# Opening a two-layer transformer kernel in four quarters of 256 features instead of two halves of 512

## The reference, cut to what matters

```
mod = silu(c) @ w_ada[0] + b_ada[0]     # 6 parts of 1024: shift, scale, gate, shift2, scale2, gate2
h   = rmsnorm(x, norm_g[0, 0]) * (1 + scale) + shift
# hgrn2_mixer(h, w_in, ...): 8 heads; w_in has 5 fields of 8 x 128 columns
q, v, zf, zb = (h @ w_in[:, f, head, :] for f in (0, 1, 2, 3))
ff, fb = sigmoid(zf), sigmoid(zb); kf, kb = 1 - ff, 1 - fb
# then a scan over the tokens in both directions, with q, k, v and the forget gates
```

## Time and profile before

| what | value |
|---|---|
| median of 3 runs | 1183.71 us (1177.64 to 1186.02) |
| span of the profiled execution | 1179.7 us |
| the median above that span | 4.0 us |
| TensorE busy in the span | 1110.8 us, 94% |
| VectorE, ScalarE, GpSimd busy | 414.1, 229.0 and 128.1 us |
| moved by DMA | 321.26 MB, 272 GB/s on average |

### The profile page before, as it was taken

One profiled execution on the slowest core, in us unless ns is written; L12 is line 12 of the kernel. 1 busy time (PEld: TensorE's weight loads), 2 busy tenths in 40 slices (PEclk: granted clock), 3 DMA queues, 4 the chain that ended last, 5 costly groups with the idle time before them and its releaser, 6 DMA issues.

```text
span 1179.7 us, 19786 instructions
## 1 busy us (share of the span) xinstructions
PE 1110.8 (94%) x8488; PEld 659.2 (56%) x8488; DVE 414.1 (35%) x1058; ACT 229.0 (19%) x530; POOL 128.1 (11%) x226
## 2 busy tenths in 40 slices
PE   4999999998999999999998899989989899999996
PEld 2666666665444666666563444434545756666552
DVE  2155555655712340000113654307843320000104
ACT  3111101101211411111111311126632311111110
POOL 0343433433100000000002000000000000000003
PEclk9999999999999999999999999999999899999999
DMA  9985444446941579999999942246751499999996
GB/s 345 307 277 157 115 144 144 144 144 216 379 160 67 179 277 422 426 426 426 427 424 339 389 167 76 89 161 215 282 218 44 155 378 429 426 425 424 426 418 228
DMA packets 101888, 321.26 MB, mean 272 GB/s; under 512 B 3985, under 2 KB 39105, under 8 KB 86433
## 3 DMA queue, kind: packets, MB, share of 16 engines
q1 hardware_dynamic: 93296, 298.05, 66.0%
q0 software_dynamic: 3248, 10.87, 2.7%
q10 hardware_dynamic: 5248, 10.98, 2.4%
HBM read 305.73 MB, written 14.16 MB: 271 GB/s over the span
## 4 chain that ended last, share of the span: by engine, by line
PE 74%; DMA 15%; DVE 4%; issue 2%; ACT 2%; SPq 2%; POOL 1%; POOLq 0%; ACTq 0%; DVEq 0%
PE bank L741 14%; PE bank L893 11%; PE bank L1088 11%; DMA ring<-in_moe_w_down 8%; PE bank L636 7%; PE bank L763 6%; PE bank L730 4%; PE bank L902 4%; PE bank L1019 4%; PE bank L531 3%; DMA ring<-in_moe_w_up 3%; DMA ring<-in_w_ada 2%; PE bank L918 2%; PE bank L622 1%; DMA ring<-expert_rows,moe_row 1%
## 5 line engine op out<-in xcount | busy, mean ns | idle before, releaser
L741 PE MATMUL bank<-ring,xn 128*64 128x256 f32 x1536 | 170.3, 380 | 4.6 <-DMA ring<-in_moe_w_up 4.2
L741 PEld LDWEIGHTS bank<-ring,xn 128*64 128x64 f32 x1536 | 110.0, 137 | 67.8 <-DMA ring<-in_moe_w_up 7.3
L893 PE MATMUL bank<-uT,ring 128*128 128x384 f32 x384 | 135.0, 496 | 0.0
L1088 PE MATMUL bank<-ring,uT 128*128 128x512 f32 x288 | 128.7, 601 | 4.6 <-DMA ring<-in_attn_w_qkv 3.0
L1802 DVE TENSOR_TENSOR moe_hh<-xn,bank 128x256 f32<-128x256 f32 x32 | 13.5, 421 | 299.0 <-ACT xn L1281 298.9
L1088 PEld LDWEIGHTS bank<-ring,uT 128*128 128x128 f32 x288 | 54.0, 192 | 69.0 <-issue 64.7
L893 PEld LDWEIGHTS bank<-uT,ring 128*128 128x128 f32 x384 | 69.3, 190 | 41.2 <-issue 1.1
L763 PE MATMUL bank<-ring,xn 128*64 128x512 f32 x384 | 85.5, 596 | 1.8 <-ACT xn L1287 1.6
L636 PE MATMUL bank<-ring,uT 128*128 128x512 f32 x192 | 84.0, 593 | 0.0
L730 PE MATMUL bank<-moe_g,moe_h 128*128 128x128 f32 x672 | 82.5, 281 | 0.8 <-DVE moe_g L1692 0.8
L730 PEld LDWEIGHTS bank<-moe_g,moe_h 128*128 128x128 f32 x672 | 78.7, 195 | 5.8 <-issue 5.8
(11 more groups left out here) (289 smaller groups left out, 1304.2 us busy)
## 6 DMA issues: line engine op xcount, KB each, us to landing
ring<-in_w_ada SPq DMA_DIRECT2D x24, 2048.0 KB, 10.0
ring<-in_moe_w_gate SPq DMA_DIRECT2D x24, 2048.0 KB, 18.5
ring<-in_moe_w_up SPq DMA_DIRECT2D x24, 2048.0 KB, 22.2
ring<-in_moe_w_down SPq DMA_DIRECT2D x20, 2048.0 KB, 25.2
ring<-in_hgrn_w_in SPq DMA_DIRECT2D x32, 512.0 KB, 7.8
moe_ring<-in_moe_w_gate SPq DMA_DIRECT2D x8, 2048.0 KB, 22.3
moe_ring<-in_moe_w_up SPq DMA_DIRECT2D x8, 2048.0 KB, 25.3
moe_ring<-in_moe_w_down SPq DMA_DIRECT2D x8, 2048.0 KB, 21.6
```

Of the source, the lines that this page charges most:

```text
L741: last = mm(bank[2 + e][64 * g:64 * g + 64, 256 * part:256 * part + 256], m["xe"][:, k, 64 * e:64 * e + 64], cols(slot)[:, k, 256 * g:256 ...
L893: last = mm(to[:, 0:TOK], w[:, k, f, :], uT[:, k, :], start=(k == 0), stop=(k == KC - 1))
L1088: last = mm(bank[b % 2][:, :], uT[:, k, t * P:(t + 1) * P], cols(slot)[:, k, :], start=(k == 0), stop=(k == KC - 1))
```

## The change

The opening now works on quarters of 256 features. `quarter(q)` loads 256 columns of the shift and 256 of the scale (1 MB each, rows of 1 KB), and `head0(q)` loads chunks 2q and 2q+1 of head 0's four fields (two loads of 256 KB, rows of 512 B). The order is quarter 0, x, head 0's rows 0, then quarter and rows of 1, 2, 3. One product now holds shift and scale of a quarter side by side in bank 6 (16 matmuls of 256 columns), and one turn and one pass of VectorE (`first_columns`) make its `mod`. The transposes of x go quarter by quarter to banks 4 and 5, and the four fields of head 0 accumulate in banks 0 to 3 across the quarters. TensorE's order in each quarter: zf, next product, zb, q, next turn, next transposes, v.

ScalarE copies product 0 before it squares x, loads the sigmoid table right after the roots, and for head 0 makes the sigmoids of zf and zb before the copy of q, so VectorE and GpSimd get a wait for q in `scan`. VectorE modulates tiles 1 and 2 in one instruction of 256 columns. GpSimd's small loads wait for head 0's last rows. Some semaphores are used a second time (`FIRST`), so that later counts on them rise by 32. The core of the diff:

```diff
-            ada(0, 0, 0, 0)
-            ada(0, 2, 2, 0)
-            ada(0, 1, 1, 0)
-            first_head((0, 2), first_in)
-            ada(0, 3, 3, 0)
-            first_head((3, 1), full[0][4])
+            head0(0)
+            for q in range(1, QUARTERS):
+                quarter(q)
+                head0(q)
@@ quarter(0) now stands ahead of the two loads of x
+            def quarter(q):
+                src = a["w_ada"][0].rearrange("(p k) (b n) -> p k b n", k=KC, b=12)
+                here = slice(256 * (q % 2), 256 * (q % 2) + 256)
+                for part in range(2):
+                    slot, blk = QUARTER_SLOTS[q][part], 2 * part + q // 2
+                    landed = full[0][slot] if q % 2 == 0 else quarter_in[q]
+                    sp.dma_start(cols(slot)[:, :, here], src[:, :, blk, here]).then_inc(landed, 16)
+            def head0(q):
+                src = a["hgrn_w_in"][0].rearrange("(k p) (f h n) -> p k f h n", p=P, f=5, h=HEADS)
+                for k in (2 * q, 2 * q + 1):
+                    sp.dma_start(head_cols(4)[:, k, :, :], src[:, k, 0:4, 0, :]).then_inc(head0_in[q], 16)
@@ TensorE
-            first_block(0, raw)
-            first_turn(0, raw)
-            first_block(1, raw)
-            first_features(0)
-            first_turn(1, raw)
-            first_block(2, raw)
-            first_features(1)
+            FIRST_FIELDS = (2, 3, 0, 1)
+            first_product(0)
+            first_turn(0)
+            first_features(0)
+            for q in range(QUARTERS):
+                first_proj(q, FIRST_FIELDS[0])
+                if q < QUARTERS - 1:
+                    first_product(q + 1)
+                first_proj(q, FIRST_FIELDS[1])
+                first_proj(q, FIRST_FIELDS[2])
+                if q < QUARTERS - 1:
+                    first_turn(q + 1)
+                    first_features(q + 1)
+                first_proj(q, FIRST_FIELDS[3])
-            proj(0, 0, 0, 0)
-            first_turn(2, raw)
-            first_block(3, raw)
-            proj(0, 0, 0, 2)
-            first_turn(3, raw)
-            proj(0, 0, 0, 4)
-            for part in (1, 3, 5, 6, 7, 8):
-                proj(0, 0, 0, part)
@@ ScalarE
+            act.wait_ge(small_in, 48)
+            root_table()
+            first_raw(0)
             act.wait_ge(x_in, 32)
             for t in range(T):
                 square(0, "squares", t)
                 root(0, "squares", "root", t)
+            gate_table()
@@ GpSimd
-            pool.wait_ge(full[0][3], 16)
+            pool.wait_ge(full[0][4], 32)
```

More of the change, by code:

```diff
@@ L236, in trunk @@
         y_out = sem("y_out")
+        FIRST = 32
+        quarter_in = [None, y_out, None, hg["state_out"]]
+        head0_in = [first_in, at["cache_in"], at["out"], full[0][4]]
         norm_act, norm_dve, root_done, x_pooled = sem("norm_act"), sem("norm_dve"), sem("root_done"), sem("x_pooled")
@@ L442, in expert_weights @@
                     sp.wait_ge(at["av"], HEADS * T)
-                    sp.wait_ge(at["out"], 32)
+                    sp.wait_ge(at["out"], FIRST + 32)
                 name, e = PARTS[part]
@@ L543, in turn_mod, with first_product @@
                 turn_rows(raw, b, to).then_inc(S[n]["mod_T"], 1)
-            def first_block(at, raw):
-                if at >= 1:
-                    need(pe, 0, "mod_raw", at)
-                ada_block(FIRST_BLOCKS[at], 0, 6)
-            def first_turn(at, raw):
-                if at >= 1:
-                    need(pe, 0, "mod_cols", at)
-                turn_mod(0, None, raw, at % 2, 7, at + 1)
-            def first_features(half):
-                for t in range(T):
-                    need(pe, 0, "xn_ready", t + 1)
-                    for j in range(4):
-                        k = 4 * half + j
-                        last = nc.tensor.transpose(bank[3 + t][:, j * P:(j + 1) * P], xn[:, t, k * P:(k + 1) * P], ident)
-                    last.then_inc(S[0]["xT_done"], 1)
+            def first_product(q):
+                if q >= 1:
+                    need(pe, 0, "mod_raw", q)
+                here = slice(256 * (q % 2), 256 * (q % 2) + 256)
+                for part in range(2):
+                    slot = QUARTER_SLOTS[q][part]
+                    if q % 2 == 0:
+                        pe.wait_ge(full[0][slot], 16)
+                    else:
+                        pe.wait_ge(quarter_in[q], 32)
+                    for r in range(2):
+                        for g in range(4):
+                            last = mm(bank[6][32 * g:32 * g + 32, 256 * part:256 * part + 256], cT[:, 2 * g + r, :],
+                                      cols(slot)[:, 2 * g + r, here], start=(r == 0), stop=(r == 1))
+                    if part == 0 and q % 2 == 1:
+                        last.then_inc(used[0][slot], 1)
+                last.then_inc(first_mm, 1)
+                if q % 2 == 1:
+                    pe.drain().then_inc(used[0][slot], 1)
@@ new lines, in first_proj @@
+            def first_proj(q, f):
+                if f == FIRST_FIELDS[0]:
+                    need(pe, 0, "uT_act", q + 1)
+                    need(pe, 0, "uT_dve", q + 1)
+                    pe.wait_ge(head0_in[q], 32)
+                w = head_cols(4)
+                for k in (2 * q, 2 * q + 1):
+                    if f == 1:
+                        for t in range(T):
+                            last = mm(bank[3][:, t * P:(t + 1) * P], uT[:, k, t * P:(t + 1) * P], w[:, k, 1, :],
+                                      start=(k == 0 and t == 0), stop=(k == KC - 1 and t == T - 1))
+                    else:
+                        last = mm(bank[(0, None, 1, 2)[f]][:, 0:TOK], w[:, k, f, :], uT[:, k, :],
+                                  start=(k == 0), stop=(k == KC - 1))
+                if q == QUARTERS - 1:
+                    last.then_inc(used[0][4] if f == 1 else hg["qzz"], 1)
@@ L1333, in _ @@
+            for q in range(QUARTERS):
+                if q >= 1:
+                    first_raw(q)
+                need(act, 0, "mod_ready", q + 1)
+                need(act, 0, "xT_done", q + 1)
+                for i in range(2):
+                    k = 2 * q + i
+                    last = A(uT[:, k, 0:P], bank[4][:, i * P:(i + 1) * P], ACT.Identity,
                              bias=mod[:, 0, k, 0:1], scale=mod[:, 1, k, 0:1])
-                last.then_inc(S[0]["uT_act"], half + 1)
+                last.then_inc(S[0]["uT_act"], 1)
@@ L1408, in _ @@
             turned_out(0, 2, 0)
[L1409 removed]
+            act.wait_ge(hg["state_out"], FIRST + 16)
             second_square(0, 0)
@@ L1510, in _ @@
             turned_out(1, 2, 0)
-            act.wait_ge(at["out"], 32)
+            act.wait_ge(at["out"], FIRST + 32)
             second_square(1, 0)
@@ L1888, in _ @@
+            first_columns(0)
             for t in range(T):
                 normalise(0, "root", "xn_ready", t)
[L1890 to L1907 removed]
@@ new lines, in _ @@
+            for q in range(QUARTERS):
+                if q >= 1:
+                    first_columns(q)
+                need(dve, 0, "mod_ready", q + 1)
+                need(dve, 0, "xT_done", q + 1)
+                for i in range(2):
+                    k = 2 * q + i
+                    last = v.tensor_scalar(uT[:, k, P:TOK], bank[5][:, 2 * i * P:(2 * i + 2) * P],
+                                           mod[:, 1, k, 1:2], mod[:, 0, k, 1:2], ALU.mult, ALU.add)
+                last.then_inc(S[0]["uT_dve"], 1)
@@ L2123, in _ @@
                 if u == 2:
-                    dve.wait_ge(at["out"], 32)
+                    dve.wait_ge(at["out"], FIRST + 32)
                 if u >= 1:
```

127 lines of the change are left out of this document (64 added, 63 removed).

## The result

The changed kernel takes 1188.34 us (median of 8 runs, 1185.90 to 1191.33), the kernel before 1184.22 (8 runs, 1177.64 to 1187.25). The ratio is 1.004, 95% interval 1.0022 to 1.0059: 4.7 us slower, with 2.6 to 7.0 as bounds (the medians differ by 4.1). The forecast was 1183.3 in a range up to 1188.0, so the time lies 0.3 us outside it, on the slow side, where I had forecast a small gain.

What follows compares the result with a forecast made beforehand. TensorE bounds the opening from 28.27 us on; head 0 ends at 22.6 + 28.95 + 2.0 = 53.6, but head 1's landing sets `following(0)` at 55.5 against 55.95 (-0.4). Span 1179.3 plus 4.0 gives 1183.3 us, range 1178.5 to 1188.

Steps and rivals of the forecast that it cites:

- Behind the opening a microsecond is worth a microsecond: From 110 to 295 us TensorE is busy 181.68 of 185 us, so a shift of the start passes on whole.
- the change in time is therefore the shift of the first matmul of `following(0)`: The whole effect equals how far that matmul moves: from 55.95 to 55.5, -0.4 us.
- `FIRST` only moves counts: Semaphores used a second time: among the edits priced at nothing.
- something outside the opening: Chance of 0.04 left over for effects elsewhere in the kernel, with no size given.
- The start of quarter 1: Opening: x lands at 14.5, `uT` of quarter 0 is ready at 20.0, product 1 starts at 22.6.
- The cost of the low level: Opening from 22.6 on: TensorE at 1.2 GHz until 24.5 to 28.9, costing 0.9 to 3.1 us, taken as 2.0.
- The work of TensorE: Opening: unchanged work, 8.35 us per quarter and 28.95 from product 1 to head 0's end; short matmuls add few tenths or nothing.
- Head 1 binds by a little: Before `following(0)`: head 1's last load lands at 55.4, after TensorE could start at 54.8.
- no change in sum: GpSimd's eleven small loads, some 6 us later but still in front of head 1's last load: priced at nothing.
- Rival 2: Head 1 late: 1 KB rows cost as at 512 B, `following(0)` 3.6 us later, 1187.3 us; chance 0.20.
- Rival 1: Opening loads: 1 KB rows cost nothing extra, gain 1.1 to 2.2 us, 1181.3 to 1182.6; chance 0.22.
- Rival 3: Opening: TensorE at the low level until 30, costing 3.7 instead of 2.0, +0.5 us, 1184.2; chance 0.09.

Runs made afterwards that it cites:

- delay: The kernel before with seven more 128-column matmuls on TensorE right before scan 0, not part of the computation: 1186.72 us, 1.0019.
- after_again: The changed kernel repeated without alteration, against the kernel before: 1189.03 us, 1.0038.
- after_pad: The changed kernel with 19 never-executed matmuls in an untaken branch of layer 0's experts: 1184.03 us, 1.0008 against the kernel before.
- rows_1k: The kernel before with each of its first four w_ada blocks loaded as two loads of 256 columns (1 KB rows): 1186.18 us, 1.0011.
- norm_first: The changed kernel with x loaded ahead of quarter 0 and the norm ahead of product 0 on each engine: 1188.68 us, 1.0054.
- before_pad: The kernel before with 32 never-executed matmuls in an untaken branch of layer 0's experts: 1184.85 us, 1.0012.
- before_pad34: The kernel before with 34 never-executed matmuls in an untaken branch of layer 0's experts: 1192.37 us, 1.0072.
- x_first: The changed kernel with both loads of x issued ahead of quarter 0: 1190.60 us, 1.0051 against the kernel before.
- before_look: The kernel before once more, with no change, for a second profile: one run, 1176.89 us.
- busy_again: A repeat of norm_small_busy, unaltered: 1179.94 us, 0.9980 against the kernel before.
- norm_small_pad: norm_small with 19 never-executed matmuls in an untaken branch of layer 0's experts: 1183.42 us, 0.9996 against the kernel before.
- norm_small_busy: norm_small with 19 executed 128-column matmuls, not part of the computation, in TensorE's waits before product 1: 1180.52 us, 0.9983 against the kernel before.
- norm_small: norm_first with GpSimd's eleven small loads moved between its scans: 1187.27 us, 1.005 against the kernel before.

## Why the prediction was wrong

Two steps failed. The larger part is outside the opening; the sign of the opening was wrong as well.

**The step that failed most: "Behind the opening a microsecond is worth a microsecond", from which "the change in time is therefore the shift of the first matmul of `following(0)`".** The first half holds as far as the profiles show (the shift of 1.6 us is unchanged at 270; delay fits it but doesn't prove it). The conclusion doesn't: the edit has an effect of its own elsewhere. "`FIRST` only moves counts" was my price for the rest of the program, and I had no term for the length of TensorE's program. The runs put in its place: a break of 3.1 us in the transposes between the layers, worth 2.9 us in the profiles and 3.5 by the ratios of after_again and after_pad. This is the 0.04 that I had left for "something outside the opening". No rival named it.

The accounting: four profiles of the changed opening start following at 57.54, 57.70, 57.03 and 56.96, those of the old one at 55.93, 55.95, 55.96 and 56.26. That is +0.7 to +1.8 us. With 2.9 to 3.5 us from the gap it makes 3.6 to 5.3, against 4.7 measured and 4.5 in the repeat. after_pad, where only the opening is left, has 1.0008, 0.9 us (between 1.4 less and 3.2 more than the kernel before).

**The opening, term by term** (time from the profiles of the changed kernel):

| step | forecast | measured |
|---|---|---|
| x landed | 14.5 | 15.25 |
| xn ready | 18.5 | 20.46 |
| `uT` of quarter 0 | 20.0 | 22.3 |
| quarter 1 landed | 22.2 | 23.09 |
| product 1 starts | 22.6 | 25.24 |
| low level from there on | 2.0 | 1.3 |
| TensorE's work behind product 1 | 28.95 - 1.85 = 27.1 | 27.59 busy of 27.88 |
| head 0 ends | 53.6 | 56.36 |
| row cost of four quarters | 2.0 | 2.5 (rows_1k) |
| head 1 landed | 55.4 | 57.1 |
| following starts | 55.5 | 57.54 |

- *The start of quarter 1* is the term that turned the sign. I let ScalarE square "the last two tiles" behind the landing of x, but it waits for both loads of x before it takes the first (`act.wait_ge(x_in, 32)`, and 15.27 is its first square), so all three stand behind it, 1.37 us each. A row that I had in hand says so: the first square of the old kernel, at 7.67, is released by the load of the sample. With x 0.75 us later that is 2.0 us in xn, and 2.6 in product 1.
- *The cost of the low level* was right in kind and place. Product 1 ran low (3.24 us) and the rest at the higher level, which came at about 27.9, inside my 24.5 to 28.9. From product 1 on it cost less than I said, since product 1 started later. Together with the low first zf it is 2.7 us; I had that one at the low level in the 22.6.
- *The work of TensorE* was right to 2%: a quarter takes 8.5 us (from product 2 at 35.23 to product 3 at 43.70), where I counted 8.35. The "few tenths" for short matmuls are there.
- *Products 2 and 3 without a wait for DMA*, and a TensorE full from then on: right.
- *Head 1 binds by a little*: wrong in this kernel, it lands 0.4 us before need; the wait "of half a microsecond" that I promised is not in the profile, the first matmul of following stands directly behind L956. As a mechanism it is right, and norm_first shows it at 2.63 us. Both limits came late, TensorE by 2.7 us (57.5 against 54.8) and head 1 by 1.7. For head 1 the rows are not all: with them alone it lands at 55.7 (rows_1k), in the changed kernel at 57.1. I had priced the small loads, which now go out from 41.4 on, at "no change in sum"; without them it lands at 53.0. So their new place is the likely rest, though no run moves them by themselves. Rival 2's own condition, 2.4 us of added row cost, was even met (2.5 in rows_1k; 349 GB/s in the window of the changed kernel, 338 to 350 in others), but it was worked out against a TensorE that would be there at 53.6.
- *Rival 1, short rows for free,* is out: 2.5 us in rows_1k. The Trainium skill ("DMA: Bandwidth & Descriptors", Specifications) puts the least transfer for full rate at 512 B, and these rows of 1 KB fall short of it, by the 2.5 us. The estimate of 1.0 us that I made from its section "Why small descriptors are slow (HBM only)" is too low.
- *Rival 3* had the sign of the opening's loss (+0.5), but by the wrong cause: TensorE was not low for longer, it started later.
- *The time itself* was tied to a span with 4.0 us around it. This was 2 us too much by the runs, and by chance made no great difference, since the kernel before came out at 1184.22.

**What stays open.** That the break is TensorE waiting for its program is inferred. For it: the profile gives no releaser, only "issue", and instructions that are never executed move it. In the 3.08 us of the changed kernel fall one transfer of 0.02 MB on queue q8 and one of 0.01 MB on q14, both called instruction queues; but the same two fall behind the start of the transposes in the kernel before and in after_pad, whose transposes don't break. So the transfers are there in any case, and what differs would be how far TensorE gets before it needs what they bring. All nine profiles with a break fit this: TensorE goes on 1.3 to 1.8 us after the transfer on q8 has ended, wherever the break lies (after 1.40, before_pad 1.50, before_pad34 1.68, rows_1k 1.80). By what count the break moves, no run shows. A stall of the same kind, 2.45 us, stands at 291.5 us in the changed kernel and in x_first, but not in after_again, so I give it no part in the loss. Nor can I part, in what the gap costs, the break itself (1.6 us between after_again and after_pad, 1.7 between the changed kernel and the one before) from what the clock takes behind it: 6.8 or 10.2 us at the lower level, against 0 to 6.8 in unbroken profiles. And since the runs lose more by the break than the profiles of the same kernels show, some of its price may lie elsewhere.

## What to carry to other kernels

An edit costs what it does where it stands and what it does to the program's layout; with a few dozen instructions more or fewer on an engine, look at every stall that ends with "issue", and repeat the kernel with never-executed instructions added before you believe a difference of half a per cent. In an opening, put each engine's instructions in the order in which their data land (ScalarE's norm behind a copy that is not ready cost more than a late x), and when a limit is removed, look for the next one right behind it. Overlap pays only if the engine is there in time: the forecast needs the whole chain up to its first steady work, tile by tile.

## What the runs showed that I had not expected

- TensorE can stand for 3.1 to 4.3 us in straight code, released by nothing that the profile shows. 34 matmuls that never run made it and cost 8.5 us of 1184, where 32 cost 1.4; 19 took it away and gave back 3.5.
- Around a break that holds up the projection the clock is at its lower level for longer: for 10.2 us in six profiles and for 6.8 in the changed kernel's. Of the seven unbroken profiles two have none there (before_look, busy_again), three have 3.4 (before, after_pad, delay) and two 6.8 (norm_small_pad, norm_small_busy).
- Rows of 1 KB: 338 to 350 GB/s, against 376 to 386 with 2 KB and 299 to 309 with 512 B.
- Eleven small loads of GpSimd ahead of a 512 KB load delay it by 4.1 us (57.1 against 53.0), though they hold only 373 KB, which at 300 GB/s would be 1.3 us.
- 19 matmuls of 128 columns in waits bring the higher level to about 12.4 us, from 27.9 in the changed kernel and about 24 in norm_small, where product 1 takes 2.18 us. Against norm_small they give back 1.3 us of the opening, which then waits for data.
